# Top-k attention: index products inside the key blocks, low weight parts on GpSimd, and the division by the sums moved behind the values

## What is computed

```python
def dsa_attention(h, w_in, cq_g, w_uq, w_uq_idx, q_g, k_g, w_out, cos, sin):
    c_q, k, v, k_idx, w_idx = jnp.split(h @ w_in, ...)
    c_q = rms_norm(c_q, cq_g)
    q = (c_q @ w_uq).reshape(B, S, H, d)                    # 16 heads of 64
    q_idx = apply_partial_rope((c_q @ w_uq_idx)..., cos, sin)   # 8 index heads of 64
    k_idx = apply_partial_rope(rms_norm(k_idx)..., cos, sin)
    ...
    def block(args):                                         # 128 queries
        dots = jnp.einsum('bqhe,bke->bqhk', qib, k_idx)
        score = jnp.einsum('bqh,bqhk->bqk', wb, jax.nn.relu(dots))
        score = jnp.where(mask, score, -jnp.inf)
        vals, idx = lax.top_k(score, topk)                   # 128 keys of up to 512
        ...
        s = jnp.einsum('bqhd,bqkhd->bhqk', qb, kg)
        p = jax.nn.softmax(jnp.where(valid[:, None], s, -jnp.inf), axis=-1)
        return jnp.einsum('bhqk,bqkhd->bqhd', p, vg)
    return o @ w_out
```

## Time and profile before

| | us |
|---|---|
| median of 3 runs | 2397.44 (2397.02 to 2399.76) |
| the profiled run, its own time | 2399.06 |
| its span in the trace | 2397.3 |
| PE busy | 2292.8 (96%) |
| DVE busy | 1264.1 (53%) |
| ACT busy | 773.8 (32%) |
| POOL busy | 133.6 (6%) |
| `lo` on DVE, line 260, mean | 2.29 |
| `hi` on ACT, line 252, mean | 1.90 |

### The profile page before, as it was taken

One profiled execution on the slowest core, in us unless ns is written; L12 is line 12 of the kernel. 1 busy time (PEld: TensorE's weight loads), 2 busy tenths in 40 slices (PEclk: granted clock), 3 DMA queues, 4 the chain that ended last, 5 costly groups with the idle time before them and its releaser, 6 DMA issues.

```text
span 2397.3 us, 28421 instructions
## 1 busy us (share of the span) xinstructions
PE 2292.8 (96%) x11616; PEld 1848.8 (77%) x11616; DVE 1264.1 (53%) x1534; ACT 773.8 (32%) x1003; POOL 133.6 (6%) x93
## 2 busy tenths in 40 slices
PE   6999999989999999999988999999999779999998
PEld 5888888867788887877865888888867547888887
DVE  5444445577544345574567544344567763634443
ACT  3222234335322323342246322122334453312221
POOL 2000001030100100120000100000100001000000
PEclk8999999999999999999989999999999899999999
DMA  4323223320232332232320232332233101223321
GB/s 143 103 90 96 97 79 95 100 75 2 79 101 92 93 99 88 88 106 88 93 67 1 71 105 88 105 101 92 66 101 89 54 1 45 97 95 98 105 88 70
DMA packets 192320, 200.54 MB, mean 84 GB/s; under 512 B 6178, under 2 KB 187520, under 8 KB 192226
## 3 DMA queue, kind: packets, MB, share of 16 engines
q1 hardware_dynamic: 192226, 199.22, 26.2%
HBM read 191.93 MB, written 2.10 MB: 81 GB/s over the span
## 4 chain that ended last, share of the span: by engine, by line
PE 87%; DVE 9%; ACT 2%; issue 1%; SPq 0%; DMA 0%; POOL 0%; DVEq 0%; ACTq 0%
PE psum L594 85%; DVE w_lo L260 1%; DVE sm L2164 1%; ACT free_h L1262 1%; PE psum L1048 1%; ACT w_hi L252 1%; DVE h_lo L1705 0%; DVE arena L1702 0%; DVE free_x L1702 0%; DVE free_h L1705 0%; DVE free_h L1709 0%; ACT arena L1262 0%; DVE sm L2245 0%; DVE buf_a L1702 0%; DVE rstd L2247 0%
## 5 line engine op out<-in xcount | busy, mean ns | idle before, releaser
L594 PE MATMUL psum<-xg_lo,w_hi 128*128 128x512 f32 x1568 | 610.2, 392 | 1.6 <-DVE xg_lo L1702 1.6
L594 PE MATMUL psum<-xg_hi,w_hi 128*128 128x512 f32 x1520 | 597.2, 393 | 3.0 <-DVE w_lo L260 2.6
L594 PE MATMUL psum<-xg_hi,w_lo 128*128 128x512 f32 x1520 | 594.0, 391 | 0.0
L252 ACT ACTIVATE w_hi<-w_raw 128x2048 fp32r<-128x2048 f32 (+1 forms) x183 | 348.2, 1903 | 492.0 <-PE psum L594 492.0
L260 DVE TENSOR_TENSOR w_lo<-w_raw,w_hi 128x2048 fp32r<-128x2048 f32 (+1 forms) x183 | 419.1, 2290 | 165.2 <-ACT w_hi L252 164.8
L594 PE MATMUL psum<-h_hi,w_hi 128*128 128x512 f32 x1144 | 452.2, 395 | 4.4 <-DVE w_lo L260 2.5
L594 PE MATMUL psum<-h_hi,w_lo 128*128 128x512 f32 x1144 | 446.3, 390 | 0.0
L594 PE MATMUL psum<-h_lo,w_hi 128*128 128x512 f32 x1144 | 446.1, 390 | 0.0
L594 PEld LDWEIGHTS psum<-xg_lo,w_hi 128*128 128x128 f32 x1568 | 295.5, 189 | 68.2 <-issue 7.7
L594 PEld LDWEIGHTS psum<-xg_hi,w_hi 128*128 128x128 f32 x1520 | 287.1, 189 | 68.0 <-issue 5.8
L594 PEld LDWEIGHTS psum<-xg_hi,w_lo 128*128 128x128 f32 x1520 | 287.0, 189 | 60.3
(11 more groups left out here) (292 smaller groups left out, 2137.3 us busy)
## 6 DMA issues: line engine op xcount, KB each, us to landing
w_raw<-in_mlp_w SPq DMA_DIRECT2D x64, 1024.0 KB, 5.2
w_raw<-in_ffn_w_gate SPq DMA_DIRECT2D x22, 1024.0 KB, 5.3
w_raw<-in_ffn_w_up SPq DMA_DIRECT2D x22, 1024.0 KB, 5.4
w_raw<-in_ffn_w_down SPq DMA_DIRECT2D x16, 1024.0 KB, 5.0
w_raw<-in_diff_w_in SPq DMA_DIRECT2D x12, 1024.0 KB, 5.1
w_raw<-in_w_in SPq DMA_DIRECT2D x9, 1024.0 KB, 5.1
w_raw<-in_dsa_w_in SPq DMA_DIRECT2D x9, 1024.0 KB, 5.2
w_raw<-in_ffn_w_down SPq DMA_DIRECT2D x8, 768.0 KB, 4.3
```

Of the source, the lines that this page charges most:

```text
L252: e.activation(w_hi[:, c % 2, 0:n], w_raw[:, c % 2, 0:n], ACT.Copy).then_inc(sem("hi_done"), 1)
L594: return pe.matmul(out, lhsT, rhs, start=start, stop=stop)
```

## The change

Five edits, all in the last attention layer.

1. Index products: n=2 starts in c+5 (two pairs) and ends in c+6 (two pairs), n=3 stands in c+6 as four pairs; c+7 has none. ACT's and DVE's order follow: `hi` of c+7 behind all of `relus(2)` and a square, `relus(3)` ahead of `uq_tile`, sums 2 and 3 directly behind each other with rounds of n=1 and the key evacuation between. The score row of n=3 moves from `rstd` to two half rows.
2. The low parts of blocks c+10 to c+13 are made by GpSimd in four pieces each, and each waits also for the next block's load.
3. The probabilities are not divided. `exp` puts its sums into `sums3`; per four units DVE takes one reciprocal, PE spreads it (`spread_sums`, a product with the identity) over bank 7, ACT copies that to `buf_d`, DVE multiplies the values of bank 6 by it into `buf_c` (`divide`), and high and low parts are made from there. All values use bank 6.
4. Seven instead of two rounds of n=3 are placed before the unit loop, and one each behind units 3 and on, none behind 0 to 2.
5. `hi` of c+13 stands at unit 6 instead of 3, and DVE waits for the load of c+15 before the residual.

The core of the diff:

```diff
@@ PE
-                    pe.wait_ge(*use(name, "_prob", u + 1))
+                    pe.wait_ge(*use(name, "_exp" if dsa else "_prob", u + 1))
...
+                    elif dsa and u % NT == 0:
+                        pe.wait_ge(sem("a3_raw"), u // NT)
...
+                def spread_sums(q):
+                    if q == 0:
+                        pe.wait_ge(sem("n0_oc"), 2)
+                    else:
+                        pe.wait_ge(sem("a3_rows"), q)
+                    pe.wait_ge(sem("a3_recip"), q + 1)
+                    for i in range(8):
+                        cc = i % 2
+                        last = mm(bank[7][HD * cc:HD * cc + HD, i // 2 * P:(i // 2 + 1) * P],
+                                  recip3[:, q % 2, i:i + 1].to_broadcast([P, HD]), ident[:])
+                    last.then_inc(sem("a3_spread"), 1)
...
                     transposes(u)
+                    if dsa and u % NT == 3:
+                        spread_sums(u // NT)
                     if u >= 1:
                         values(u - 1)
...
-                if k == 6:
+                if k == 4:
                     gn_stat("sk", 1)
+                if k >= 6:
+                    dots(2, (2 * k - 12, 2 * k - 11))
             def in_k3(k):
-                if 1 <= k < 5:
-                    dots(2, (2 * k - 2, 2 * k - 1))
+                if k < 2:
+                    dots(2, (2 * k + 4, 2 * k + 5))
+                elif k < 6:
+                    dots(3, (2 * k - 4, 2 * k - 3))
             def in_uq(t):
-                dots(3, (t,))
-                if t == 3:
+                if t == 2:
                     gn_stat("sk", 3)
@@ ACT
                 def out_tile(g):
-                    act.wait_ge(*use(name, "_pv", 4 * (g + 1)))
                     if dsa:
+                        act.wait_ge(sem("a3_raw"), g + 1)
...
+                    if dsa and u % NT == 3:
+                        act.wait_ge(sem("a3_spread"), u // NT + 1)
+                        a(buf_d[:, u // NT % 2, :], bank[7], ACT.Copy).then_inc(sem("a3_rows"), 1)
-                    if dsa and u == 3:
+                    if dsa and u == 6:
                         hi(act, at["dsa"] + 13)
...
             relus(1)
-            hi(act, c + 7)
-            relus(2, (0, 1))
+            relus(2)
             act.wait_ge(sem("evac"), c + 6)
             gn_square("sk", 2)
-            relus(2, range(2, 8))
+            hi(act, c + 7)
+            relus(3)
@@ DVE
+                def recips(q):
+                    dve.wait_ge(*use(name, "_exp", NT * q + 4))
+                    dve.reciprocal(recip3[:, q % 2, :], sums3[:, q % 2, :]).then_inc(sem("a3_recip"), 1)
+                def divide(q):
+                    dve.wait_ge(*use(name, "_pv", NT * q + 4))
+                    dve.wait_ge(sem("a3_rows"), q + 1)
+                    if q >= 2:
+                        dve.wait_ge(*use(name, "_oc", q - 1))
+                    tt(buf_c[:, q % 2, :], bank[6], buf_d[:, q % 2, :], ALU.mult).then_inc(sem("a3_raw"), 1)
...
-                    norm(u)
+                    if not dsa:
+                        norm(u)
                     if u + 2 < len(units):
                         smax(u + 2)
+                    if dsa and u % NT == 2:
+                        recips(u // NT)
+                    if dsa and u % NT == 0 and u:
+                        divide(u // NT - 1)
...
+            def in_sum3(hh):
+                if hh in (0, 1, 5):
+                    take(1, 1)
+                if hh == 3:
+                    lo(dve, c + 7)
+            index_sum(3, between=in_sum3)
             take(1, 2)
...
             evac_scaled(c + 6, k2[:, 6:8, :])
...
+            take(1, 4)
+            lo(dve, c + 8)
+            take(1, 2)
+            gn_rsqrt("sk")
+            take(1, 16)
+            mask(1)
...
-            lo(dve, c + 12)
+            take(3, 3)
             pairs_attention("a3", True, early=True)
-            take(3, 2)
+            take(3, 4)
             def top(u):
-                if u == 0:
+                if u == 1:
                     dve.wait_ge(sem("kmask_done"), 2)
                     first_lo(1)
-                if u == 3:
-                    lo(dve, c + 13)
-                elif u <= 13:
-                    take(3, 2 if u == 13 else 1)
+                if u >= 3:
+                    take(3, 1)
@@ GpSimd
+            def lo_parts(c):
+                pool.wait_ge(sem("hi_done"), c + 1)
+                pool.wait_ge(sem("lo_done"), c)
+                pool.wait_ge(sem(f"landed{(c + 1) % 2}"), 16 * ((c + 1) // 2 + 1))
+                for q in range(4):
+                    part = slice(q * S, (q + 1) * S)
+                    last = pool.tensor_tensor(w_lo[:, c % 2, part], w_raw[:, c % 2, part], w_hi[:, c % 2, part].bitcast(F32),
+                                              ALU.subtract)
+                last.then_inc(sem("lo_done"), 1)
+            for b in range(10, 14):
+                lo_parts(at["dsa"] + b)
             fin(7)
```

More of the change, by code:

```diff
@@ L1541, in out_tile @@
                 def out_tile(g):
-                    act.wait_ge(*use(name, "_pv", 4 * (g + 1)))
                     if dsa:
+                        act.wait_ge(sem("a3_raw"), g + 1)
                         n, g0 = 1 + g // 2, 4 * (g % 2)
-                        a(h2_hi[:, g0:g0 + 4, n * P:(n + 1) * P], bank[6 + g % 2].rearrange("p (a q) -> p a q", q=P),
+                        a(h2_hi[:, g0:g0 + 4, n * P:(n + 1) * P], buf_c[:, g % 2, :].rearrange("p (a q) -> p a q", q=P),
                           ACT.Copy).then_inc(use(name, "_hi")[0], 1)
                     else:
+                        act.wait_ge(*use(name, "_pv", 4 * (g + 1)))
                         a(q2[:, g, :], bank[6 + g % 2], ACT.Copy).then_inc(use(name, "_oc")[0], 1)
@@ L2189, in out_tile @@
                     part = slice(n * P, (n + 1) * P)
-                    tt(h2_lo[:, g0:g0 + 4, part], bank[6 + g % 2].rearrange("p (a q) -> p a q", q=P),
+                    tt(h2_lo[:, g0:g0 + 4, part], buf_c[:, g % 2, :].rearrange("p (a q) -> p a q", q=P),
                        h2_hi[:, g0:g0 + 4, part].bitcast(F32), ALU.subtract).then_inc(use(name, "_oc")[0], 1)
@@ L2207, in pairs_attention @@
                 if dsa:
+                    divide(len(units) // NT - 1)
                     out_tile(len(units) // NT - 1)
@@ L2219, in _, with halves, score_row @@
             stats(6)
+            def halves(n, v):
+                return v.rearrange("p (a k) -> p a k", a=2) if n == 3 else v
+            def score_row(n):
+                row = index_score[n]
+                return (row, row[:, 1, P:2 * P]) if n == 3 else (row[:, 0:(n + 1) * P], row[:, n * P:(n + 1) * P])
             def index_sum(n, between=None):
                 w = (n + 1) * P
-                sc = index_score[n][:, 0:w]
+                sc, last = score_row(n)
                 for hh in range(8):
@@ L2227, in index_sum @@
                     if hh == 0:
[L2228 removed]
+                        ts(sc, halves(n, buf_c[:, u % 2, 0:w]), widx[:, n, 0:1], None, ALU.mult).then_inc(sem("dot_acc"), 1)
                     else:
                         dve.wait_ge(sem("dot_acc"), u)
[L2231 removed]
+                        stt(sc, halves(n, buf_c[:, u % 2, 0:w]), widx[:, n, hh:hh + 1], sc, ALU.mult, ALU.add).then_inc(sem("dot_acc"), 1)
                     if between:
@@ L2234, in index_sum @@
                 dve.wait_ge(sem("dot_acc"), 8 * n)
-                link(tt(sc[:, n * P:], sc[:, n * P:], chunk_mask, ALU.add))
+                link(tt(last, last, chunk_mask, ALU.add))
             took = {1: 0, 2: 0, 3: 0}
             def take(n, rounds):
-                sc = index_score[n][:, 0:(n + 1) * P]
+                sc = score_row(n)[0]
                 for j in range(took[n], min(took[n] + rounds, TOPK // 8)):
@@ L2309, in _ @@
             dve.reciprocal(rs_q[:], bank[4][:, P:2 * P].rearrange("p (n r) -> p n r", r=32)[:, :, 0:16]).then_inc(sem("rs_q"), 1)
-            lo(dve, c + 10)
-            take(2, 1)
+            take(2, 2)
             def first_max(h):
@@ L2337, in _ @@
             first_max(1)
-            take(2, 2)
-            lo(dve, c + 11)
-            take(2, 1)
+            take(2, 4)
             first_norm(1)
```

62 lines of the change are left out of this document (26 added, 36 removed).

## The result

| | before | after |
|---|---|---|
| median, us | 2397.90 (2397.02 to 2399.76, 4 runs) | 2366.58 (2366.10 to 2367.91, 4 runs) |
| span of the profiled run | 2397.3 | 2364.9 |
| PE busy | 2292.8 | 2282.6 |
| DVE busy | 1264.1 | 1241.8 |
| POOL busy | 133.6 | 154.7 |

The changed kernel takes 0.9868 of the time before (95% interval 0.9853 to 0.9884), 31.3 us less; forecast were 29, 2368.5 us.

A forecast was written before the change was run, and what follows sets the result against it. PE was taken as bound by last-attention waits, mainly for DVE's scaled probabilities. Attention 79.8 us plus allowances made 85.3 against 111.4, gaining 26.1; index products added 2.5, sum 28.6, called 29: 2368.5 us, own range 2361 to 2376 (0.60).

The forecast's parts named there:

- the attention at 83 to 88 us: Sign of being right: the last attention stage takes 83 to 88 us, against 111.4 before.
- spread groups of 0.6 us: Sign of being right: in the last attention, eight-fold groups of spread matmuls on PE take 0.6 us each.
- The bound: Last attention: of 111.4 us, 33 are PE waits, 26.6 of them for the scaled probabilities; gain 26.1 us.
- DVE's queue from the maximum of unit 5 to the mask, 37.2 us: Last attention: DVE's operations and waits, summed in order over this stretch, take 37.2 us; PE's work there is about 31.
- the sum was 79.8: Last attention before allowances: 8.8 us ahead of DVE's queue, 37.2 in it, 33.8 of PE behind the mask.
- The allowances, 5.5 us: Added to the attention: 2 us lower clock after the mask's wait, 1 another spell, 1 handoffs, 1.5 GpSimd.
- The spread products: Last attention: eight added PE matmuls per four units take 0.6 us, six groups 3.6 us.
- GpSimd: Low parts moved there take 5.2 us a block, blocks 10 and 11 have 11 us; cost zero, 1.5 us DVE interference allowed.
- Index products, gain 2.5 predicted: Index stage: pairing saves 4.6 us of PE work, waits take part back; gain 2.5 us, bounds -2 and 5.5.
- The rope product's wait: Index stage: PE's next wait of 0.9 us, for a rope product, goes.
- PE-paced: Rival, chance 0.17: DVE waits overlap better than the in-order sum; attention 75 us, gain 36, time 2357.
- Cold clock: Rival, chance 0.15: PE gaps in units 4 to 15 keep it at 1.2 GHz, 11 us lost instead of 3; 2379.

The follow-up runs named there:

- the tripled kernel: Changed kernel with each GpSimd low-part subtraction made three times in a row; 2387.40 us, ratio 0.9952 to the kernel before.
- the pair of traces above: Two traces of one kernel, the changed kernel with DVE's subtraction of the output's low part one unit later; 2359.44 us, repeated 2360.64 us.

## Why the prediction was right, and where it was off

**The total.** Forecast were 29 us, measured 31.3. The total is nearer than its parts: the attention gave 4.4 us more than forecast (30.5 against 26.1), the index stage 2.1 less (0.4 against 2.5), and the two errors cancel in part. That the size came out this close is in part luck; the mechanism of the attention is not. Of the signs of being right that the prediction lists, two did not come: the attention at 83 to 88 us (80.9) and spread groups of 0.6 us (0.93).

**The bound.** Right. The attention gave 30.5 of the 32.4 us of span, and without the division, all else kept, it gave 7.8. Waits of PE for `norm` gone, the units behind the mask 3.50 us apart where no spread stands between (transposes at 1940.42 and 1943.92), two waits for reciprocals and one for the mask.

**DVE's queue from the maximum of unit 5 to the mask, 37.2 us.** This was the term that decided. The trace has 1888.36 to 1925.02, 36.7 us, with nine rounds, eleven maxima, and three waits for ACT's high part of 1.79, 2.00 and 2.17 us, where 1.9 each were taken. The waits for values before a division, 1.2 in the sum, did not come; DVE waited 0.65 and 0.20 for scores. Before it 8.5 us (predicted 8.8), behind it from 1925.16 on 35.6 (predicted 33.8). With 0.1 between them these make 80.9; the sum was 79.8.

**The allowances, 5.5 us.** Mostly not needed. Two us for the lower clock behind the mask and one for another spell: the clock was 1.00 in both traces of this kernel. It does come in other runs: in two whose edits leave the attention alone it cost 1.8 us there (82.7 against 80.9). One was for handoffs, 1.5 for GpSimd, of which 0.6 came. The attention came out at 80.9 instead of 85.3 us.

**The spread products, mis-sized.** The sum had 0.6 us for eight, read from a values group of "x8" in the earlier trace rows. The group has 16 records, 1.09 us long, 0.93 to the next start:

```profile
1943.92 1.04 PE L1050 MATMUL psum<-ident,free_h 128*128 128x128 f32 x8
1944.88 1.09 PE L596 MATMUL psum<-ident,recip 128*64 128x128 f32 x16
1945.81 1.04 PE L596 MATMUL psum<-free_h,arena 128*64 128x128 f32 x16
1946.78 1.13 PE L596 MATMUL psum<-arena,free_x 64*128 64x512 f32 x4
```

One product of these leaves two records, so "x8" in the earlier trace rows was four products. Six groups cost 5.6 us instead of 3.6; three of them, 1.0 us together too much, stand behind the mask and are more than half of the 1.8 missing there.

**GpSimd.** Right. Blocks of 5.47, 5.04, 5.03 and 4.98 us, no PE wait for them, a slack of 10.8 us for block 10 as the tripled kernel shows. What the prediction did not say is how much it pays: DVE's subtractions back in place cost 10.3 us. It wrote of them as 4.5 us that pay for the rounds; three of them ahead of the loop cost 3.8 us at the start of the stage, and the one in the loop, with 3.17 us of waiting for its high part, most of the 4.9 up to the mask. In two places the engines met. In the attention a multiply of 128x2 took 0.78 us (1905.37) beside block 13, against 0.16 for the others, 0.6 us of the 1.5 allowed. Ahead of it a sum of the rotary part, 128x512 with both inputs in SBUF, took 1.70 us (1840.47) beside block 10, against 0.69 in the kernel before (1842.59); R to S does not show it, 127.24 us against 127.20 with these low parts on DVE. The Trainium skill, page "SBUF — State Buffer", section "Who interferes with whom", says that a DVE instruction with two SBUF inputs and a GpSimd instruction that reads SBUF exclude each other, and that one with at most one SBUF input, outside DVE's two-port modes, is not held up; the trace agrees on both, since MAX8 beside the same block took 0.68 as elsewhere.

**Index products, gain 2.5 predicted, 0.4 measured.** The pairs are right: 1.13 us for a pair of 512 columns (1782.89), once 1.61 behind a wait of 0.16 for ACT. Their waits were right too: PE's 0.71 and 1.20 us in the up-projection (0.9 and 1.4 forecast), its end at 1810.70, which is 1812.4 on the time axis of the kernel before, whose R is 1.7 us later (1811.9 forecast), and the wait for the reciprocals at 1.82 (1.9 forecast). So the step behind it starts 1.05 us earlier than before instead of 1.7. The rope product's wait of 0.86 went, as said. The rest was lost behind the wait of 1.82: clock 0.72 for 6 us, where the kernel before has 1.00, which costs 1.5 us by the pair of traces above; 1.05 + 0.86 - 1.5 is the 0.4 that was measured. The step that failed is that a wait of 1.8 us was counted as 1.8: of the nine traces that have it eight have the clock of 0.72 behind it, and of the five with about 1.25 or none there, none has. In the ninth, at full clock, the stage gained 1.96 us, near the forecast. Taking the wait away gave 2.04 us in the stage. Why a wait of this length is mostly, but not always, followed by the lower clock stays open.

**The rivals.** PE-paced, 75 us in the attention: not here; with DVE's standing still gone the stage is 73.6 us, so the figure was near what PE needs. Cold clock: not found in the attention. That DVE overlaps better than an in-order sum was wrong: the queue ran as summed.

## What to carry to other kernels

When a handoff through a loaded engine is removed, sum that engine's whole queue in order, up to the last result that others need, with its own waits in it; the sum hit the queue within 0.5 us. Then look in that queue for the instruction that waits longest for a third engine, and put it one step later: one moved line gave 7 us here, where moving the reciprocal that PE's wait named gave none. Split a stage at the last result that others need before saying why two gains do not add. Count products by their records before pricing a new group by an old one.

## Of the hardware, not expected

A stretch at the lower clock can move rather than vanish. In the two kernels without the wait of 1.82 us, and with clock 1.00 from 1814 to 1820, the first 7 us of the attention have 0.76; of the eleven other traces of altered kernels only that with GpSimd tripled has this there. So an index stage that gained 2.0 us had brought nothing by E. What ties the two places together no run here shows. The length of the wait does not decide alone: behind the mask's wait of 3.1 us the clock stays at 1.00 in both traces of the changed kernel, and in the run with the index products as before it is 0.84 there. One program can have such a stretch in one execution and not in another (125.69 and 127.19 us for the same stage), so a difference of 1.5 to 2 us between single traces is to be read with the clock beside it.
